# Two weight tiles of a convolution layer split by GpSimd, more convolution taps on VectorE and fewer on TensorE

## The chip, the cores and the metric

The kernel runs on one core of a Trainium2 chip. The metric is the device time of one execution in microseconds (us). The engines are TensorE (PE in the profile, its weight loads PEld), VectorE (DVE), ScalarE (ACT), GpSimd (POOL) and SyncE (SP), which here only issues transfers.

## The reference, cut to what matters

The model is a two-layer decoder trunk over 272 prompt positions and 32 sample positions (304 columns, D = 1024). Layer 0 is a pooling mixer and a dense SwiGLU, layer 1 is the Conformer convolution module below and a top-2-of-8 mixture of experts.

```python
def conv_module(x, prev, w1, b1, dw, dwb, lng, lnb, w2, b2):
    h = jnp.dot(x, w1) + b1                 # first pointwise layer, 1024 -> 2048
    a, gt = jnp.split(h, 2, axis=-1)
    u = a * jax.nn.sigmoid(gt)
    ext = jnp.concatenate([prev.astype(u.dtype), u], axis=1)
    c = lax.conv_general_dilated(ext, dw.astype(ext.dtype)[:, None, :], window_strides=(1,), padding='VALID',
                                 dimension_numbers=('NWC', 'WIO', 'NWC'), feature_group_count=D_MODEL)
    c = layer_norm(c + dwb, lng, lnb)       # 31 taps for each of the 1024 channels
    y = jnp.dot(jax.nn.silu(c), w2) + b2    # second pointwise layer
    return y.astype(x.dtype), ext[:, -CONV_CTX:]
```

## The kernel before, in words

**Split products.** Features lie on the 128 partitions in blocks (8 blocks make D), positions along the free axis. Each matrix product of the layers is made from three products of rounded parts: a weight tile of 128x2048 lands in `raw`, ScalarE rounds it to `w_hi` (`hi(t)`, L699), VectorE makes the low half `w_lo = raw - w_hi` in place over `raw` (`lo(t)`, L1357), and TensorE multiplies high by high, high by low and low by high. `raw` is a ring of slots, `w_hi` has 6 buffers. Weight tiles are numbered by t; `T_W1` = 33 to 40 are the eight tiles of the first pointwise layer, 41 to 44 those of the second, from 45 on the experts' tiles follow. The semaphore `hi_ready` counts finished high halves, `split_ready` finished low halves, `tile_used` tiles that TensorE has finished with.

**The stage around the change** has four turns, i = 0 to 3, of two tiles each (values and gates of two feature blocks, L1091 on TensorE). At the end of a turn ScalarE makes the sigmoids of the two gate blocks (L852) and VectorE writes two blocks of u (`uext`, L1585 and L1587). In the gaps between, VectorE splits the next tiles and convolves: `tap(q)` adds one tap of block q to `cacc` (the first of a block is L1536, the others L1540), and `convolve(pair, n)` makes n taps of both blocks of a pair. VectorE's order is written out by hand in this loop; each engine runs its own program in order and waits only for semaphores.

**The convolution is divided.** Blocks 0 to 3 (pairs 0 and 1) are convolved by VectorE alone, 31 taps each. Blocks 4 to 6 are convolved by TensorE with diagonal matrices (L1168): three matmuls for a tap, whose diagonals ScalarE builds beforehand (L789, L791, high and low). Block 7, `SHARED`, is divided by taps: TensorE makes taps 0 to 15, VectorE taps 16 to 30, and VectorE adds the two sums at the end (L1609). `DIAGS` lists TensorE's seven sets of diagonals, the last is that of the shared block. The samples' columns are convolved by VectorE in four groups of eight small operations (L1561).

**What follows.** When both have finished, TensorE sums the blocks for the mean of a normalization (L1030), VectorE subtracts it (L1432), ScalarE squares (L743), and so on to the second pointwise layer, the router and the experts. GpSimd's program at this point waits for the variance before the stage, zeroes the first columns of `uext` (L623), and then waits until the router to issue indirect transfers (L638, L629, L633).

The lines of VectorE's turn that matter most:

```python
            for i in range(NW1 // 2):
                if i < NW1 // 2 - 1:
                    lo(T_W1 + 2 * i + 2)
                    if i:
                        convolve(0, 4)
                    lo(T_W1 + 2 * i + 3)
                if i == NW1 // 2 - 1:
                    uc_low(0)
                    uc_low(1)
                if i:
                    convolve(0, 4 if i < NW1 // 2 - 1 else 12)
```

Of the kernel before, what the change touches and what calls it, by code (L numbers as in the profile page):

```python
# [29 lines left out]
ALU = mybir.AluOpType  # L30
# [5 lines left out]
HIGH = 6  # L36
# [5 lines left out]
def build_trunk(nc, x_prompt, x_sample, state_pool, state_conv, meta, pool_w, pool_scale, conv_w1,  # L42
# [5 lines left out]
    KC = D // P  # L48
# [5 lines left out]
    TAPS = conv_dw.shape[1]  # L54
# [17 lines left out]
    T_W1 = 3 * NJ  # L72
    NW1 = 2 * D // TW
# [13 lines left out]
    def raw_slot(t):  # L87
        if t >= T_MOE:
            return (t - T_MOE + DENSE) % RAW
        return t - T_W2 if t >= T_W2 else t % DENSE  # L90
# [9 lines left out]
    with ExitStack() as ctx:  # L100
# [18 lines left out]
        raw = [at(f"raw{i}", [P, 2048], F32, ring_at + 8192 * i) for i in range(RAW)]  # L119

        w_lo = [at(f"w_lo{i}", [P, 2048], F32R, ring_at + 8192 * i) for i in range(RAW)]
        w_hi = [at(f"w_hi{i}", [P, 2048], F32R, split_at + 8192 * i) for i in range(HIGH)]
# [71 lines left out]
        Q0 = KC - NPE  # L194
# [55 lines left out]
        def sem(name):  # L250
            return ctx.enter_context(nc.semaphore(name))
# [11 lines left out]
        u_stored = sem("u_stored")  # L263
        hi_ready = sem("hi_ready")
        split_ready = sem("split_ready")
        tile_used = sem("tile_used")
        consts_ready = sem("consts_ready")
        ctx_zeroed = sem("ctx_zeroed")
# [113 lines left out]
        def up_end(b):  # L382
# [40 lines left out]


        SHARED = KC - 1
        DIAGS = [(q, k0, min(k0 + 16, TAPS)) for q in range(Q0, KC) for k0 in (0, 16)
                 if q != SHARED or k0 == 0]
        EARLY = len(diag_at)

        def diag(j):  # L430
# [160 lines left out]
        def _(pool):  # L591
# [29 lines left out]

            pool.wait_ge(var_done, 2)
            pool.memset(uext[:, :, 0:CCTX], 0.0).then_inc(ctx_zeroed, 1)  # L623


            rows = bass.IndirectOffsetOnAxis
# [58 lines left out]
        def _(act):  # L685
# [96 lines left out]
            def diagonals(j, first, end):  # L782

                q, k0, k1 = DIAGS[j]
                n = k1 - k0
# [210 lines left out]
        def _(pe):  # L996
# [100 lines left out]
            for i in range(NJ):  # L1097
                for kind in range(2):
                    t = 2 * i + kind
# [3 lines left out]
                    for s in range(2 if t else 0):  # L1103
                        q = 2 * i + s
# [8 lines left out]
            for i in range(NJ):  # L1113
                t = T_DOWN + i
# [3 lines left out]
                for s in range(TR):  # L1118
                    for c in range(KC):
                        cols = slice(c * P, (c + 1) * P)  # L1120
                        for k, (w, x) in enumerate(((wh, h_hi), (wh, h_lo), (wl, h_hi))):
                            last = pe.matmul(ps[c][:, 0:NT], w[:, s, cols], x[i % 2][:, s, :],  # L1122
                                             start=(i == 0 and s == 0 and k == 0),
                                             stop=(i == NJ - 1 and s == TR - 1 and k == 2))
# [12 lines left out]
            for i in range(NW1 // 2):  # L1137
                for kind in range(2):
                    t = T_W1 + 2 * i + kind
                    pe.wait_ge(split_ready, t + 1)  # L1140
                    if t == T_W1:
                        last = feature_block((ps[0], ps[2]), NT, t, (0, 1), x_base=KC)
                    for s in range(2 if t > T_W1 else 0):
                        q = 2 * i + s
                        if q >= 4:
                            pe.wait_ge(u_done, q - 3)
                        last = feature_block((ps[2 * (q % 4) + kind],), NT, t, (s,))
                    last.then_inc(tile_used, 1)

            for j, (q, k0, k1) in enumerate(DIAGS):  # L1150
                c = q - Q0
                if j == 2:
                    pe.wait_ge(u_done, KC)
                    for k, (part, half) in enumerate(U_JOBS):
                        dst = ps[U_BANKS[k]]
                        for o in range(4):
                            f = 4 * half + o
                            src = uext[:, f, UP - CCTX:UP] if part == 0 else uext[:, f, UP:UEXT]
                            n = (CCTX, NS)[part]
                            last = pe.transpose(dst[0:n, o * P:(o + 1) * P], src, ident[:])  # L1160
                        last.then_inc(turned, 1)
                pe.wait_ge(uc_lo_done, c + 1)
                pe.wait_ge(diag_done, j + 1)
                dh, dl = diag(j)
                for k in range(k0, k1):
                    cols = slice((k - k0) * P, (k - k0 + 1) * P)
                    for m, (w, x) in enumerate(((dh, uc_hi), (dh, uc_lo), (dl, uc_hi))):
                        last = pe.matmul(ps[2 + c][:, 0:SEQ], w[:, cols], x[:, c, k:k + SEQ],  # L1168
                                         start=(k == 0 and m == 0),
                                         stop=(k == (15 if q == SHARED else TAPS - 1) and m == 2))  # L1170
                last.then_inc(diag_used, 1)
            pe.wait_ge(evac_a, A_U)
            norm(2)
# [1 line left out]
            for i in range(NW2):  # L1175
                t = T_W2 + i
# [14 lines left out]
            for k, (i, half) in enumerate(X_JOBS):  # L1191
                if k == 1:

                    pe.wait_ge(logits_out, 1)
                    for t in range(3):
                        m = OUT_ROWS[t]
# [148 lines left out]
        def _(dve):  # L1345
# [8 lines left out]
            def lo(t, n=None):  # L1354

                dve.wait_ge(hi_ready, t + 1 if n is None else n * TE + (t + 1))
                dve.tensor_tensor(w_lo[raw_slot(t)][:], raw[raw_slot(t)][:], w_hi[t % HIGH][:],  # L1357
                                  ALU.subtract).then_inc(split_ready, 1)


            for job, (i, half) in enumerate(IN_JOBS):
# [119 lines left out]
            for i in range(NJ):  # L1481
# [19 lines left out]
                for s in range(2):  # L1501
                    q = 2 * i + s
# [3 lines left out]
            for i in range(-1, NJ):  # L1506
                if 0 <= i < NJ - 1:
                    lo(T_DOWN + i + 2)
                if i + 1 < NJ:
                    k = (i + 1) % 2  # L1510
# [13 lines left out]

            dve.wait_ge(ctx_zeroed, 2)
            dve.wait_ge(tile_used, T_W1)
            FIRST_TAP = [0] * (KC - 1) + [16]
            taps_done = FIRST_TAP[:]
            convolved = []

# [15 lines left out]
            def convolve(pair, count):  # L1546

                for _ in range(count):
                    tap(2 * pair)
                    tap(2 * pair + 1)  # L1550
# [19 lines left out]
            for i in range(NW1 // 2):  # L1570
                if i < NW1 // 2 - 1:
                    lo(T_W1 + 2 * i + 2)
                    if i:
                        convolve(0, 4)
                    lo(T_W1 + 2 * i + 3)
                if i == NW1 // 2 - 1:
                    uc_low(0)
                    uc_low(1)
                if i:
                    convolve(0, 4 if i < NW1 // 2 - 1 else 12)  # L1580
                for s in range(2):
                    q = 2 * i + s
                    dve.wait_ge(sig_done, q + 1)
                    src = ps[2 * (q % 4)]
                    dve.scalar_tensor_tensor(out=uext[:, q, CCTX:UP], in0=src[:, 0:NPR], scalar=v(V_B1 + q),  # L1585
                                             in1=sg[s][:, 0:NPR], op0=ALU.add, op1=ALU.mult)
                    dve.scalar_tensor_tensor(out=uext_s[:, q, :, :],  # L1587
                                             in0=src[:, NPR:NT].rearrange("p (b j) -> p b j", b=SB), scalar=v(V_B1 + q),
                                             in1=sg[s][:, NPR:NT].rearrange("p (b j) -> p b j", b=SB),
                                             op0=ALU.add, op1=ALU.mult).then_inc(u_done, 1)  # L1590
                dve.wait_ge(u_done, 2 * i + 2)

            uc_low(2)
            uc_low(3)
            convolve(0, TAPS - taps_done[0])
            dve.wait_ge(conv_step, len(convolved))
            dve.tensor_copy(most[:], eps[:]).then_inc(rows_convolved, 2)
            for r in range(TAPS):
                convolve(1, 1)
                if r < TAPS - 16:  # L1600
                    tap(SHARED)
                if r % 8 == 0:
                    for c in range(KC):
                        sample_tap(c, r // 8)
# [11 lines left out]
            for i in range(NW2):  # L1616
                lo(T_W2 + 2 + i)
                dve.wait_ge(tile_used, T_W2 + i + 1)
                for s in range(2):
                    q = 2 * i + s  # L1620
# [304 lines left out]
```

## Time and profile before

| | us |
|---|---|
| median of 3 runs | 1245.68 (1245.18 to 1245.83) |
| the profiled execution, its own time | 1244.82 |
| its span in the trace | 1243.0 |
| TensorE busy | 1197.5 (96% of the span) |
| VectorE busy | 977.1 (79%) |
| ScalarE busy | 807.4 (65%) |
| GpSimd busy | 31.0 (2%) |
| mean granted clock of TensorE | 0.991 |

The times of the trace count from the start of the span. A share of busy time is a mean over stages with different limits; the stage around the change lies between 287 and 387 us. Idle time is given with the instruction that ended it, as far as the trace shows one.

### The profile page before, as it was taken

To read this page: it belongs to the slowest core of one execution; us is meant where nothing else is said; L and a number is where in the kernel's file an instruction comes from. 1 tells how busy PE (TensorE), PEld (TensorE's weight loads), DVE (VectorE), ACT (ScalarE), POOL (GpSimd) and SP (SyncE) were. 2 spreads that over 40 slices of the span, in tenths; PEclk is the share of its full clock that TensorE was granted. 3 is DMA by queue.
4 is the path that set the end of the run, shared out by engine and by line. 5 is a ranking of instruction groups with operands and counts; after the bars stand their busy time and mean duration, and the time that the engine had idled before them with its cause. 6 is when DMAs were issued, how large, how long until landed. Compare 5 with 4: busy or idle time off the path is not lost.

```text
span 1243.0 us, 16100 instructions
## 1 busy us (share of the span) xinstructions
PE 1197.5 (96%) x6538; PEld 1036.4 (83%) x6538; DVE 977.1 (79%) x918; ACT 807.4 (65%) x875; POOL 31.0 (2%) x43
## 2 busy tenths in 40 slices
PE   6899999999998979999999999999999999999995
PEld 4799999999997868888888888888888888888884
DVE  6787444447898579879889888888888888888886
ACT  4545654436496467777768768777777777777771
POOL 0000000000000000000000001001001001001000
PEclk9999999999999979999999999999999999999998
DMA  9144544442193349999999999999999999999991
GB/s 258 40 157 149 170 149 157 141 157 89 56 317 110 136 145 365 363 364 355 388 373 362 384 367 365 384 367 363 390 367 362 390 365 353 389 372 345 395 334 50
DMA packets 171533, 346.26 MB, mean 279 GB/s; under 512 B 7059, under 2 KB 59635, under 8 KB 171419
## 3 DMA queue, kind: packets, MB, share of 16 engines
q1 hardware_dynamic: 168515, 335.34, 75.3%
q0 software_dynamic: 2736, 9.19, 2.9%
q8 instruction: 54, 0.88, 0.3%
q10 hardware_dynamic: 199, 0.62, 0.2%
q14 instruction: 29, 0.23, 0.1%
HBM read 336.87 MB, written 10.44 MB: 279 GB/s over the span
## 4 chain that ended last, share of the span: by engine, by line
PE 86%; DVE 10%; ACT 2%; DMA 1%; issue 1%; POOLq 0%; SPq 0%; POOL 0%; DVEq 0%; ACTq 0%
PE bank L1259 39%; PE bank L1283 19%; PE bank L1091 18%; PE bank L1122 6%; DVE cacc L1540 3%; PE bank L1268 1%; DVE w_lo L1357 1%; PE bank L1030 1%; PE bank L1076 1%; DVE sg L1437 1%; DMA xg_rows<-rows_dram,row_in 1%; DMA xin<-in_x_prompt_dram 1%; ACT w_hi L699 0%; ACT sq L743 0%; DVE cacc L1561 0%
## 5 line engine op out<-in xcount | busy, mean ns | idle before, releaser
L1357 DVE TENSOR_TENSOR w_lo<-raw,w_hi 128x2048 fp32r<-128x2048 f32 x309 | 704.3, 2290 | 163.9 <-ACT w_hi L699 162.9
L699 ACT CAST w_hi<-raw 128x2048 fp32r<-128x2048 f32 x309 | 589.2, 1914 | 242.6 <-PE bank L1259 82.5
L1259 PE MATMUL bank<-w_hi,xg_hi 128*128 128x512 f32 (+1 forms) x768 | 293.3, 382 | 0.6 <-DVE xg_lo L1752 0.6
L1259 PE MATMUL bank<-w_lo,xg_hi 128*128 128x512 f32 (+1 forms) x768 | 289.6, 377 | 0.0
L1259 PE MATMUL bank<-w_hi,xg_lo 128*128 128x512 f32 (+1 forms) x768 | 289.4, 377 | 0.0
L1091 PE MATMUL bank<-x_hi,w_hi 128*128 128x304 f32 (+1 forms) x544 | 165.8, 305 | 6.9 <-DVE x_lo L1444 3.7
L1259 PEld LDWEIGHTS bank<-w_hi,xg_lo 128*128 128x128 f32 x768 | 144.8, 189 | 29.2
L1259 PEld LDWEIGHTS bank<-w_hi,xg_hi 128*128 128x128 f32 x768 | 144.8, 189 | 29.0 <-issue 1.0
L1259 PEld LDWEIGHTS bank<-w_lo,xg_hi 128*128 128x128 f32 x768 | 144.9, 189 | 27.9
L1091 PE MATMUL bank<-x_hi,w_lo 128*128 128x304 f32 (+1 forms) x544 | 164.1, 302 | 0.0
L1091 PE MATMUL bank<-x_lo,w_hi 128*128 128x304 f32 (+1 forms) x544 | 163.9, 301 | 0.0
L1283 PE MATMUL bank<-w_hi,ht_hi 128*128 128x512 f32 x352 | 140.1, 398 | 2.3 <-DVE ht_lo L1776 1.9
L1283 PE MATMUL bank<-w_lo,ht_hi 128*128 128x512 f32 x352 | 139.2, 396 | 0.0
L1283 PE MATMUL bank<-w_hi,ht_lo 128*128 128x512 f32 x352 | 139.2, 396 | 0.0
L1091 PEld LDWEIGHTS bank<-x_hi,w_hi 128*128 128x128 f32 x544 | 102.2, 188 | 8.9 <-issue 6.3
L1091 PEld LDWEIGHTS bank<-x_hi,w_lo 128*128 128x128 f32 x544 | 102.7, 189 | 0.0
L1091 PEld LDWEIGHTS bank<-x_lo,w_hi 128*128 128x128 f32 x544 | 102.2, 188 | 0.1
L1283 PEld LDWEIGHTS bank<-w_hi,ht_hi 128*128 128x128 f32 x352 | 66.1, 188 | 19.6 <-DVE ht_lo L1776 4.3
L1283 PEld LDWEIGHTS bank<-w_hi,ht_lo 128*128 128x128 f32 x352 | 66.1, 188 | 16.0
L1283 PEld LDWEIGHTS bank<-w_lo,ht_hi 128*128 128x128 f32 x352 | 66.1, 188 | 15.3
L1122 PE MATMUL bank<-h_hi,w_hi 128*128 128x304 f32 x176 | 54.4, 309 | 1.9 <-DVE h_lo L1514 1.9
L1540 DVE SCALAR_TENSOR_TENSOR cacc<-uext,vec,cacc 128x256 f32<-128x256 f32 x134 | 54.0, 486 | 0.0
(220 smaller groups left out, 1076.8 us busy)
## 6 DMA issues: line engine op xcount, KB each, us to landing
raw<-in_moe_w_gate_dram SPq DMA_DIRECT2D x88, 1024.0 KB, 6.6
raw<-in_moe_w_up_dram SPq DMA_DIRECT2D x88, 1024.0 KB, 7.1
raw<-in_moe_w_down_dram SPq DMA_DIRECT2D x88, 1024.0 KB, 6.8
raw<-in_conv_w_dram SPq DMA_DIRECT2D x12, 1024.0 KB, 5.2
raw<-in_ffn_w_gate_dram SPq DMA_DIRECT2D x11, 1024.0 KB, 5.4
raw<-in_ffn_w_up_dram SPq DMA_DIRECT2D x11, 1024.0 KB, 5.4
raw<-in_ffn_w_down_dram SPq DMA_DIRECT2D x11, 1024.0 KB, 4.8
sums_dram<-acc SPq DMA_DIRECT2D x3, 512.0 KB, 3.3
```

The source lines that it names most:

```text
L699: act.copy(w_hi[t % HIGH][:], raw[raw_slot(t)][:]).then_inc(hi_ready, 1)
L1030: last = pe.matmul(ps[0][:, 0:n], mean_mat[:], z(c), start=(c == first), stop=(c == end))
L1076: last = pe.matmul(ps[1][:, 0:n], mean_mat[:], sq[:, c, 0:n], start=(c == 0), stop=(c == KC - 1))
L1091: last = pe.matmul(bank[:, 0:n], w[:, c, cols], x[:, c, 0:n], start=(c == 0 and k == 0), stop=(c == KC - 1 and k == 2))
L1122: last = pe.matmul(ps[c][:, 0:NT], w[:, s, cols], x[i % 2][:, s, :], start=(i == 0 and s == 0 and k == 0), stop=(i == NJ - 1 and s == TR - ...
L1259: done = pe.matmul(bank[:, 0:w], x[:, f, :], m[:, c, :], start=(f == 0 and k == 0), stop=(f == KC - 1 and k == 2))
L1268: done = pe.transpose(ps[4 + j % 2][:, s * P:(s + 1) * P], hn[:, s * P:(s + 1) * P], ident[:])
L1283: done = pe.matmul(ps[6 + half][:, :], x[:, i * TR + s, :], w[:, s, cols], start=(j == 0 and i == 0 and s == 0 and k == 0), stop=(j == NB ...
L1357: dve.tensor_tensor(w_lo[raw_slot(t)][:], raw[raw_slot(t)][:], w_hi[t % HIGH][:], ALU.subtract).then_inc(split_ready, 1)
L1437: link(dve.reciprocal(rs[:, 0:n], rs[:, 0:n]))
L1540: ins = dve.scalar_tensor_tensor(out=out, in0=src, scalar=v(V_DW + KC * k + q), in1=out, op0=ALU.mult, op1=ALU.add)
```

## The change

GpSimd makes the low halves of tiles 38 and 40 (`POOL_TILES`) with one subtraction of 128x2048 each, and TensorE waits for `pool_split` there; VectorE's next `lo` counts `split_ready` up by two, so that the count stays that of the tiles. In the turns i = 1 and 2 VectorE makes 4 and then 7 taps of pair 0 where it made 4, a low half and 4; in turn 3 it makes the remaining 9 of pair 0 and the first 4 of pair 1 where it made 12 of pair 0. Of the shared block TensorE has 8 taps (`SHARE`) and VectorE 23, and the last set of diagonals is half as large. The taps of pair 0 behind the last turn are gone.

```diff
--- before.py
+++ after.py
@@ -263,6 +263,7 @@
         u_stored = sem("u_stored")
         hi_ready = sem("hi_ready")
         split_ready = sem("split_ready")
+        pool_split = sem("pool_split")
         tile_used = sem("tile_used")
         consts_ready = sem("consts_ready")
         ctx_zeroed = sem("ctx_zeroed")
@@ -423,8 +424,11 @@
 
 
         SHARED = KC - 1
-        DIAGS = [(q, k0, min(k0 + 16, TAPS)) for q in range(Q0, KC) for k0 in (0, 16)
+        SHARE = 8
+        DIAGS = [(q, k0, SHARE if q == SHARED else min(k0 + 16, TAPS)) for q in range(Q0, KC) for k0 in (0, 16)
                  if q != SHARED or k0 == 0]
+
+        POOL_TILES = (T_W1 + 5, T_W1 + 7)
         EARLY = len(diag_at)
 
         def diag(j):
@@ -621,6 +625,10 @@
 
             pool.wait_ge(var_done, 2)
             pool.memset(uext[:, :, 0:CCTX], 0.0).then_inc(ctx_zeroed, 1)
+            for t in POOL_TILES:
+                pool.wait_ge(hi_ready, t + 1)
+                pool.tensor_tensor(w_lo[raw_slot(t)][:], raw[raw_slot(t)][:], w_hi[t % HIGH][:],
+                                   ALU.subtract).then_inc(pool_split, 1)
 
 
             rows = bass.IndirectOffsetOnAxis
@@ -1137,7 +1145,10 @@
             for i in range(NW1 // 2):
                 for kind in range(2):
                     t = T_W1 + 2 * i + kind
-                    pe.wait_ge(split_ready, t + 1)
+                    if t in POOL_TILES:
+                        pe.wait_ge(pool_split, POOL_TILES.index(t) + 1)
+                    else:
+                        pe.wait_ge(split_ready, t + 1)
                     if t == T_W1:
                         last = feature_block((ps[0], ps[2]), NT, t, (0, 1), x_base=KC)
                     for s in range(2 if t > T_W1 else 0):
@@ -1167,7 +1178,7 @@
                     for m, (w, x) in enumerate(((dh, uc_hi), (dh, uc_lo), (dl, uc_hi))):
                         last = pe.matmul(ps[2 + c][:, 0:SEQ], w[:, cols], x[:, c, k:k + SEQ],
                                          start=(k == 0 and m == 0),
-                                         stop=(k == (15 if q == SHARED else TAPS - 1) and m == 2))
+                                         stop=(k == (SHARE - 1 if q == SHARED else TAPS - 1) and m == 2))
                 last.then_inc(diag_used, 1)
             pe.wait_ge(evac_a, A_U)
             norm(2)
@@ -1355,7 +1366,7 @@
 
                 dve.wait_ge(hi_ready, t + 1 if n is None else n * TE + (t + 1))
                 dve.tensor_tensor(w_lo[raw_slot(t)][:], raw[raw_slot(t)][:], w_hi[t % HIGH][:],
-                                  ALU.subtract).then_inc(split_ready, 1)
+                                  ALU.subtract).then_inc(split_ready, 2 if t - 1 in POOL_TILES else 1)
 
 
             for job, (i, half) in enumerate(IN_JOBS):
@@ -1524,7 +1535,7 @@
 
             dve.wait_ge(ctx_zeroed, 2)
             dve.wait_ge(tile_used, T_W1)
-            FIRST_TAP = [0] * (KC - 1) + [16]
+            FIRST_TAP = [0] * (KC - 1) + [SHARE]
             taps_done = FIRST_TAP[:]
             convolved = []
 
@@ -1572,12 +1583,15 @@
                     lo(T_W1 + 2 * i + 2)
                     if i:
                         convolve(0, 4)
-                    lo(T_W1 + 2 * i + 3)
+                    else:
+                        lo(T_W1 + 2 * i + 3)
                 if i == NW1 // 2 - 1:
                     uc_low(0)
                     uc_low(1)
                 if i:
-                    convolve(0, 4 if i < NW1 // 2 - 1 else 12)
+                    convolve(0, 7 if i < NW1 // 2 - 1 else TAPS - taps_done[0])
+                if i == NW1 // 2 - 1:
+                    convolve(1, 4)
                 for s in range(2):
                     q = 2 * i + s
                     dve.wait_ge(sig_done, q + 1)
@@ -1592,12 +1606,12 @@
 
             uc_low(2)
             uc_low(3)
-            convolve(0, TAPS - taps_done[0])
             dve.wait_ge(conv_step, len(convolved))
             dve.tensor_copy(most[:], eps[:]).then_inc(rows_convolved, 2)
             for r in range(TAPS):
-                convolve(1, 1)
-                if r < TAPS - 16:
+                if taps_done[2] < TAPS:
+                    convolve(1, 1)
+                if r < TAPS - SHARE:
                     tap(SHARED)
                 if r % 8 == 0:
                     for c in range(KC):
```

## Rows read from the trace of the kernel before

**Rows 1.** Chain that ended last, 284 to 410 us: start us, us, what.

```profile
...
287.35 54.26 PE bank L1091 x384
...
349.44 9.51 DVE cacc L1540 x24
...
382.76 4.13 PE bank L1030 x16
```

**Rows 2.** Busy us of PE, PEld, DVE, ACT, POOL by stretch; clock, DMA.

```profile
...
287.00:341.00 54.00, 53.65 (x381) 53.51 (x382) 46.20 (x90) 30.36 (x59) 0.00 (x0) 1.00 0.25 79
341.00:382.00 41.00, 41.00 (x348) 40.80 (x346) 39.66 (x122) 35.71 (x108) 0.00 (x0) 1.00 0.71 247
...
450.00:460.00 10.00, 6.47 (x40) 5.21 (x40) 6.30 (x24) 1.75 (x5) 0.95 (x1) 0.51 0.65 220
```

**Rows 3.** TensorE's timeline, first and last diagonal matmuls: start, us, what.

```profile
...
341.44 0.28 PE L1168 MATMUL bank<-uc_hi,diag_h 128*128 128x256 f32 x1
...
342.39 0.28 PE L1168 MATMUL bank<-uc_hi,diag_l 128*128 128x256 f32 x1
...
382.00 0.28 PE L1168 MATMUL bank<-uc_hi,diag_l 128*128 128x256 f32 x1
```

**Rows 4.** Timeline of VectorE, 306 to 383 us: start, us, what, idle before.

```profile
...
306.35 0.73 DVE L1536 TENSOR_SCALAR cacc<-uext,vec 128x256 f32<-128x256 f32 x2
306.99 2.46 DVE L1540 SCALAR_TENSOR_TENSOR cacc<-uext,vec,cacc 128x256 f32<-128x256 f32 x6
309.37 2.29 DVE L1357 TENSOR_TENSOR w_lo<-raw,w_hi 128x2048 fp32r<-128x2048 f32 x1
...
315.31 0.50 DVE L1585 SCALAR_TENSOR_TENSOR uext<-bank,vec,sg 128x272 f32<-128x272 f32 x1 [0.48 <-ACT sg L852]
...
317.58 2.29 DVE L1357 TENSOR_TENSOR w_lo<-raw,w_hi 128x2048 fp32r<-128x2048 f32 x1 [1.02 <-ACT w_hi L699]
319.79 3.25 DVE L1540 SCALAR_TENSOR_TENSOR cacc<-uext,vec,cacc 128x256 f32<-128x256 f32 x8
...
328.75 0.50 DVE L1585 SCALAR_TENSOR_TENSOR uext<-bank,vec,sg 128x272 f32<-128x272 f32 x1 [0.34 <-ACT sg L852]
...
330.87 9.59 DVE L1540 SCALAR_TENSOR_TENSOR cacc<-uext,vec,cacc 128x256 f32<-128x256 f32 x24
342.19 0.50 DVE L1585 SCALAR_TENSOR_TENSOR uext<-bank,vec,sg 128x272 f32<-128x272 f32 x1 [1.73 <-ACT sg L852]
...
382.39 0.15 DVE L1606 COPY mv<-eps 128x1 f32<-128x1 f32 x1
```

**Rows 5.** Timeline of ScalarE in the same stretch.

```profile
...
306.49 1.91 ACT L699 CAST w_hi<-raw 128x2048 fp32r<-128x2048 f32 x1 [2.46 <-DMA raw<-in_conv_w_dram]
...
319.88 1.91 ACT L699 CAST w_hi<-raw 128x2048 fp32r<-128x2048 f32 x1 [2.40 <-DMA raw<-in_conv_w_dram]
...
368.58 4.78 ACT L791 ACTIVATE diag_l<-ident,dw_lo 128x128 fp32r<-128x128 f32 x16
376.57 0.47 ACT L835 ACTIVATE cacc<-bank,vec 128x256 f32<-128x256 f32 x1 [2.50 <-PE bank L1168]
```

**Rows 6.** Groups of GpSimd by shape: count, busy us, mean ns, idle before.

```profile
...
L623 POOL MEMSET uext<- 128x240 f32 x1 | 0.3, 298 | 279.4 <-PE bank L1076 279.4
L605 POOL TENSOR_SCALAR_AFFINE_SELECT before<-before 128x128 f32<-128x128 f32 x1 | 0.3, 292 | 0.1
...
L597 POOL MEMSET pext<- 128x120 f32 x1 | 0.2, 196 | 0.0
```

**Rows 7.** Timeline of TensorE where its clock rises again.

```profile
...
463.11 0.63 PE L1259 MATMUL bank<-w_hi,xg_hi 128*128 128x512 f32 x1
463.54 0.55 PE L1259 MATMUL bank<-w_lo,xg_hi 128*128 128x512 f32 x1
...
464.39 0.40 PE L1259 MATMUL bank<-w_lo,xg_hi 128*128 128x512 f32 x1
464.62 0.40 PE L1259 MATMUL bank<-w_hi,xg_lo 128*128 128x512 f32 x1
```

## The prediction

> **What bounds the kernel now.** I read the chain of waits first, then the stretches of busy time, then each engine's timeline in the stage. In the chain [rows 1] the reader is to see that TensorE sets the end up to the last tile of the first pointwise layer (384 matmuls, 54.26 us from 287.35) and that VectorE's taps set it from there to 382.76, when the mean's matmuls start. The stretches [rows 2] show why it is a near tie: from 341 to 382 TensorE is busy all 41.0 us and VectorE 39.66 us, both at the full granted clock. The timelines give the two ends. TensorE's last diagonal matmul starts at 382.00 and takes 0.28, so it ends at 382.28 [rows 3]; VectorE's taps end where the small copy begins, at 382.39 [rows 4]. So neither alone is worth anything: a gain here needs both to end earlier, and it is the smaller of the two gains. The turns before 341 bind TensorE: 54.26 us for eight tiles is 6.78 us a tile, so tile 38, the sixth, is wanted at 287.35 + 5 x 6.78 = 321.3 and tile 40 at 334.8. VectorE has idle time in these turns [rows 4], GpSimd does nothing at all [rows 2].
>
> **TensorE's part.** It loses 8 taps of three matmuls. From 341.44 to 342.39 there are eight steps [rows 3], 0.119 us each, so 24 matmuls are 2.8 us and its end moves from 382.28 to 379.5. The last set of diagonals has 16 scalings in place of 32; the second half alone, 16, took 4.78 us and was over by 373.4, TensorE came to this set only at 376.5 [rows 5], so ScalarE's saving is hidden and counts for nothing. The earlier release of the experts' first slots counts for nothing either: these tiles are wanted only after the router.
>
> **VectorE's part, if GpSimd does not disturb it.** A tap costs 0.396 us (24 in 9.51 [rows 1]); the first two taps of a pair take 306.99 - 306.35 = 0.64 together [rows 4]. Turn 1: the eight taps end at 309.37, 14 more take 5.54 and end at 314.9, before the sigmoid lets VectorE go on at 315.31. Turn 2: the low half ends at 319.79, 22 taps take 8.71 and end at 328.5, before 328.75. Turn 3: from 330.87, 18 taps of pair 0 (7.13) and the first eight of pair 1 (0.64 + 6 x 0.396 = 3.02) end at 341.0, before 342.19. So no turn becomes longer, and the two low halves of 2.29 us are paid out of it and out of idle time of 0.48, 0.34 and 1.73 us. Behind the last turn there were 6 + 62 + 15 = 83 taps; now there are 54 of pair 1 and 23 of the shared block, 77. Six taps less are 2.4 us: VectorE's end moves from 382.39 to 380.0. TensorE's 379.5 is earlier, so the stage would gain 2.4 us, and nothing behind it binds differently: the mean, the square and the second layer follow in the same chain.
>
> **GpSimd's part.** Its program stands at a wait with nothing queued but transfers that come some 100 us later, so queuing behind the two subtractions costs nothing. Tile 38 is rounded at 306.49 + 1.91 = 308.4 and tile 40 at 321.8 [rows 5]; each leaves 13 us until TensorE wants it. The trace has no operation of GpSimd with two tiles as input. From below: two fills, 0.298 us for 240 columns and 0.196 for 120 [rows 6], give 0.85 ns a column, 1.8 us for 2048. From above: the selection of 128 columns takes 0.292 [rows 6]; without some 0.09 of fixed time (0.196 - 120 x 0.85 ns) that is 1.55 ns a column, 3.3 us for one operand and up to 6.4 if the second is read after the first. I take 4.6 us, close to the middle of these last two (4.8) and to sixteen selections (4.7). All of them fit into 13 us, so the wait that TensorE now has for GpSimd costs nothing unless GpSimd is held up by over 8 us.
>
> **What decides: whether the two run side by side.** While GpSimd subtracts, VectorE runs nothing but taps and low halves, each with two operands in the same memory as GpSimd's. No row here shows such a pair together: in the stage GpSimd has 0.00 us [rows 2]. The two ends are that they do not touch (0) and that each excludes the other, so that VectorE stands still for the whole of both subtractions (2 x 4.6 = 9.2 us). I take exclusion, as the likelier of two untested ends, and it is by far the larger term. Of the 9.2 us, idle time of the turns absorbs 0.4 (314.9 to 315.31), 1.0 (the low half that waits for its rounding until 317.58 [rows 4]), 0.2 (328.5 to 328.75) and 1.2 (341.0 to 342.19): 2.8 us. 6.4 us remain, and VectorE ends at 380.0 + 6.4 = 386.4, 4.0 later than before. The point from which the sign turns: 2 x H - 2.8 = 2.4, so H = 2.6 us of standstill for each tile.
>
> The Trainium skill's page "SBUF — State Buffer", section "Who interferes with whom", speaks against this change: VectorE operations with two inputs in this memory contend with a GpSimd operation that reads it, and the one that issues second blocks until the first has finished. Its page "GPSIMD Engine Reference", section 3.1, gives 4497 ns for a two-input operation of 2048 columns, an estimate of 9.0 us for both tiles. By this rule and this price the sum would be that of exclusion, 0.2 us smaller; no trace so far shows either.
>
> **What is late next under exclusion.** In the delayed turns the u blocks come 4 to 7 us later; ScalarE's later diagonals slip by as much but were ready several us early (the last set by 3 us, and it is now 4.7 us shorter). TensorE never waits for them, ends at 379.5, and then idles 7.2 us before the mean's 16 matmuls. Before the experts, where TensorE was busy for 6.47 of 10 us, the granted clock had a mean of 0.51, the 1.2 GHz level [rows 2]; there a matmul came each 0.43 us (463.11 to 463.54) and at 2.4 GHz each 0.23 (464.39 to 464.62) [rows 7], 1.85 times as long. The 4.13 us of mean matmuls [rows 1] at the lower level would take 3.5 us more; between 0 and 3.5 I take 2.0, as the clock may rise inside the group.
>
> **The sum.** -2.4 + 6.4 + 2.0 = +6.0 us: a span of 1249.0, an execution of 1244.82 + 6.0 = 1250.8. The profiled execution is 0.9 below the median of the runs, so against the median it is 1245.7 + 6.0 = 1251.7.
>
> **The rivals.**
> *Side by side.* GpSimd's reads do not hold VectorE up. For it: nothing in the trace shows GpSimd disturbing VectorE. Against it: nothing there reads two tiles at once on both. Then the gain is 2.4 us, 1243.3: not slower, the other side of my forecast. It decides when the standstill is under 2.6 us a tile.
> *GpSimd has to wait for VectorE's gaps.* Taps follow each other closely (0.396 us apart), so a waiting GpSimd may come in only where VectorE stops. Tile 38 then runs from 314.9 to 319.5, under the writes of u, which read a bank and one tile; the low half at 317.58 slips 1.9 us, 22 taps end at 330.45, the writes of u end at 331.7, and tile 40 runs from 330.45 to 335.05, 0.2 us after TensorE wants it. The remaining work starts at 335.05 and reaches the last writes of u at 346.1 in place of 342.19, 3.9 late. VectorE ends at 383.9, 1.5 after the old end: 1247.2, and up to 1250.7 with the slower clock. An even sharing of the reads, in which both become slower, lands in the same place.
> *The subtraction is shorter or longer than I take.* With exclusion and 1.8 us there is a loss of 0.9 and a gain of 1.5 in all; with 6.4 us a loss of 10.0 and +7.6, with the clock +11.1.
>
> **How the numbers follow.** A measurement of this kernel tells about 0.2%, 2.5 us, from no change. Exclusion has 0.50, gaps or sharing 0.14, side by side 0.36. Exclusion is slower by over 2.5 us in nearly all its cases (0.47), gaps in a third (0.05): slower 0.52. Side by side stands 0.1 us short of the bound, so four in ten of it count as faster (0.15) and the rest as same (0.21); with gaps (0.09) and a short standstill (0.03) same has 0.33. The forecast is 1251.7; its own range is 1247 (one operand's 3.3 us, full clock) to 1255 (clock low throughout, a longer subtraction). The range for 8 in 10 reaches to side by side, from 1242.8 to 1254.8.
>
> **What would show it.** Right: in turns 1 and 2 one tap or low half of VectorE stretched to about 4.6 us, or a hole as long before it, beside each subtraction of GpSimd; the last writes of u near 349 in place of 342.19; taps to about 386; an idle TensorE from 379.5, with the granted clock under 1.00 in the mean's matmuls. Wrong: taps still 0.396 apart beside GpSimd, last writes of u at 342.2, both engines ready near 380. A subtraction of over 13 us would be wrong in another way: TensorE would then wait for tile 38 or 40, and the loss would stand before 341.

## The result, and the profile after

The changed kernel takes 1249.74 us (median of 9 runs, 1246.52 to 1252.69) and the kernel before, run on the same chips, 1245.18 (9 runs, 1244.39 to 1246.4). The ratio is 1.0036, with a 95% interval of 1.0024 to 1.0047: slower by 4.5 us. The profiled execution has a span of 1248.8 us and 1250.65 in all, 5.8 us more than that of before.

The chain that ended last, from 284 to 412 us in the changed kernel, passes to VectorE earlier and stays there longer:

```profile
...
286.94 27.37 PE bank L1099 x192
...
317.19 4.04 DVE w_lo L1368
321.22 13.07 DVE cacc L1551 x22
...
336.41 7.13 DVE cacc L1551 x18
...
382.57 1.59 DVE cacc L1551 x4
...
384.61 6.46 PE bank L1038 x16
```

Against [rows 1] the reader sees three things. TensorE leaves the chain after four tiles (27.37 us), not eight. A low half that took 2.29 us is in it with 4.04, and 22 taps that would take 8.7 with 13.07. The 16 matmuls of the mean, 4.13 us before, take 6.46.

GpSimd's two subtractions and VectorE's timeline beside them:

```profile
...
308.23 10.84 POOL L630 TENSOR_TENSOR w_lo<-raw,w_hi 128x2048 fp32r<-128x2048 f32 x1 [25.44 <-ACT w_hi L707]
321.56 4.92 POOL L630 TENSOR_TENSOR w_lo<-raw,w_hi 128x2048 fp32r<-128x2048 f32 x1 [2.49 <-ACT w_hi L707]
```

```profile
...
306.57 8.01 DVE L1551 SCALAR_TENSOR_TENSOR cacc<-uext,vec,cacc 128x256 f32<-128x256 f32 x20
...
317.19 4.04 DVE L1368 TENSOR_TENSOR w_lo<-raw,w_hi 128x2048 fp32r<-128x2048 f32 x1 [1.05 <-ACT w_hi L707]
321.14 13.15 DVE L1551 SCALAR_TENSOR_TENSOR cacc<-uext,vec,cacc 128x256 f32<-128x256 f32 x22
...
346.48 0.50 DVE L1599 SCALAR_TENSOR_TENSOR uext<-bank,vec,sg 128x272 f32<-128x272 f32 x1
...
384.25 0.15 DVE L1620 COPY mv<-eps 128x1 f32<-128x1 f32 x1
```

```profile
...
321.94 4.83 DVE L1551 SCALAR_TENSOR_TENSOR cacc<-uext,vec,cacc 128x256 f32<-128x256 f32 x1
```

The last row is the only instruction of VectorE that runs from 322 to 326: one tap of 4.83 us among taps of 0.48, beside GpSimd's second subtraction of 4.92. Beside the first one, which has a record of 10.84 us, no tap is longer than usual (20 in 8.01). The low half behind these taps starts at 317.19, GpSimd is done at 319.07, and the low half ends 2.16 us after that, at 321.23: it stood still until GpSimd was done and then took about its own 2.29 us. The last writes of u begin at 346.48 in place of 342.19 [rows 4].

The stretches (busy us of PE, PEld, DVE, ACT, POOL, then TensorE's granted clock) and TensorE's last diagonal matmul:

```profile
...
287.00:341.00 54.00, 54.00 (x384) 53.84 (x385) 47.23 (x87) 26.55 (x46) 15.75 (x2) 1.00 0.25 79
341.00:382.00 41.00, 38.01 (x321) 37.60 (x319) 40.96 (x124) 34.63 (x105) 0.00 (x0) 1.00 0.75 257
382.00:387.00 5.00, 2.39 (x5) 1.85 (x6) 4.80 (x12) 0.00 (x0) 0.00 (x0) 0.55 1.04 385
```

```profile
...
378.73 0.28 PE L1179 MATMUL bank<-uc_hi,diag_l 128*128 128x256 f32 x1
384.61 1.78 PE L1038 MATMUL bank<-cacc,mean_mat 128*128 128x288 f32 x3 [5.60 <-DVE mv L1621]
```

TensorE has finished at 379.0 and waits 5.6 us for VectorE; its granted clock is 1.00 up to 382, as in [rows 2], and has a mean of 0.55 from 382 to 387, for the most part the 1.2 GHz level.

### The profile page after: what moved, and what is told of

Its sections match the earlier page's. It is cut to its first block, busy times and chain, and to the rows that moved or that the text cites. A ratio compares the mean times of both kernels' runs of the same rounds, so it can differ in the third digit from the quotient of the medians.

```text
span 1248.8 us, 16045 instructions
## 1 busy us (share of the span) xinstructions
PE 1198.6 (96%) x6514; PEld 1037.0 (83%) x6514; DVE 982.1 (79%) x924; ACT 802.4 (64%) x859; POOL 47.0 (4%) x45
## 4 chain that ended last, share of the span: by engine, by line
PE 84%; DVE 12%; ACT 2%; DMA 1%; issue 1%; POOLq 0%; POOL 0%; DVEq 0%; ACTq 0%
PE bank L1270 39%; PE bank L1294 19%; PE bank L1099 16%; PE bank L1130 6%; DVE cacc L1551 4%; DVE w_lo L1368 2%; PE bank L1279 1%; PE bank L1038 1%; PE bank L1084 1%; DVE sg L1448 1%; DMA xg_rows<-rows_dram,row_in 1%; ACT w_hi L707 1%; ACT sq L751 0%; DVE cacc L1572 0%; PE bank L1018 0%
## 5 line engine op out<-in xcount | busy, mean ns | idle before, releaser
L1551 DVE SCALAR_TENSOR_TENSOR cacc<-uext,vec,cacc 128x256 f32<-128x256 f32 x142 | 61.4, 521 | 0.0
```

The costliest lines, as they stand in the source:

```text
L1551: ins = dve.scalar_tensor_tensor(out=out, in0=src, scalar=v(V_DW + KC * k + q), in1=out, op0=ALU.mult, op1=ALU.add)
```

## The experiments

All are compared by one length that the start of the stage does not shift: from the first matmul of tile 33 to the copy behind VectorE's last tap. In the kernel before it is 382.39 - 287.35 = 95.04 us, in the changed one 384.25 - 286.94 = 97.31, so VectorE is 2.3 us later. A span in the table is that of one execution. Since the times of the changed kernel alone lie 6.2 us apart, the readings rest on these lengths and not on the spans.

| kernel | VectorE's end against before | mean's matmuls, us | span or ratio |
|---|---|---|---|
| before | 0 | 4.1 | 1243.0 |
| changed | +2.3 | 6.5 | ratio 1.0036 (1.0024 to 1.0047) |
| the same, second profile | +2.4 | 6.2 | span 1245.7 |
| one column on GpSimd | -2.4 | 4.1 | ratio 0.997 (0.9958 to 0.9981) |
| fill on GpSimd | -2.4 | 4.1 | span 1240.7 |
| copy on GpSimd | -2.2 | 4.1 | span 1240.7 |
| tile 40 alone | +0.5 | 6.9 | span 1246.7 |
| eight pieces | +2.6 | 5.8 | span 1247.4 |
| one subtraction at the start | +2.3 | 6.1 | ratio 1.0014 (1.0004 to 1.0025) |
| asked in mid-stream | +1.0 | 6.6 | span 1249.3 |
| asked at the gaps | +1.5 | 6.7 | span 1246.9 |
| matmuls to keep TensorE busy | +2.3 | 4.1 | ratio 1.0023 (1.0011 to 1.0036) |
| 16 taps of the shared block again | -0.5 | 4.1 | ratio 1.0005 (0.9994 to 1.0015) |
| idle time filled, no GpSimd | -1.6 | 4.1 | ratio 0.9993 (0.9983 to 1.0002) |

**Is it GpSimd's reading?** First its work taken away:

```diff
-                pool.tensor_tensor(w_lo[raw_slot(t)][:], raw[raw_slot(t)][:], w_hi[t % HIGH][:],
+                pool.tensor_tensor(w_lo[raw_slot(t)][:, 0:1], raw[raw_slot(t)][:, 0:1], w_hi[t % HIGH][:, 0:1],
                                    ALU.subtract).then_inc(pool_split, 1)
 ...
-                wh, wl = wide(w_hi[t % HIGH]), wide(w_lo[raw_slot(t)])
+                wh, wl = wide(w_hi[t % HIGH]), wide(w_hi[t % HIGH] if t in POOL_TILES else w_lo[raw_slot(t)])
```

> The changed kernel, but GpSimd subtracts one column of each of its two tiles and TensorE takes the high half in place of the low one there, so the low halves of tiles 38 and 40 are left out. Exclusion: without GpSimd's long reads VectorE's taps stay 0.396 us apart, they end 2.4 us earlier than in the kernel before (near 380), TensorE does not idle and keeps its clock, and the time is 2.4 us below that of the kernel before (0.2% faster). Rival (the new order of taps and TensorE's shorter part cost the time, not GpSimd): it stays 4 to 6 us above the kernel before.

```profile
...
308.76 8.00 DVE L1551 SCALAR_TENSOR_TENSOR cacc<-uext,vec,cacc 128x256 f32<-128x256 f32 x20
...
321.59 8.80 DVE L1551 SCALAR_TENSOR_TENSOR cacc<-uext,vec,cacc 128x256 f32<-128x256 f32 x22
```

```profile
...
310.31 6.51 POOL L630 TENSOR_TENSOR w_lo<-raw,w_hi 128x1 fp32r<-128x1 f32 x1 [25.34 <-ACT w_hi L707]
```

The taps are back at 20 in 8.00 and 22 in 8.80 us, VectorE's end is 2.42 us earlier than before, and the time 0.3% lower (the 2.4 us are 0.2%, at the edge of the interval). So the order of the taps and TensorE's eight taps, with two low halves that no engine makes, gain what the sum without GpSimd said; the loss is that of GpSimd's subtractions. The record of 6.51 us for one column ends at 316.82, 0.06 us behind the last tap of turn 1 (308.76 + 8.00 = 316.76), which matters below. Then its work with no input, and with one:

```diff
+                pool.memset(w_lo[raw_slot(t)][:].bitcast(F32), 0.0).then_inc(pool_split, 1)   # the fill
+                pool.tensor_copy(w_lo[raw_slot(t)][:], raw[raw_slot(t)][:]).then_inc(pool_split, 1)   # the copy
```

> The changed kernel, but GpSimd fills its two tiles with zeros, which writes 128x2048 and reads nothing; the low halves of tiles 38 and 40 are left out. Exclusion between two readers: no tap or low half of VectorE is stretched, taps end near 380, span 2.4 us below that of the kernel before. Rival (any long work of GpSimd in this memory stops VectorE): a tap or low half is stretched by about the length of the fill, 1.8 us, twice, less the idle time of the turns, and the span is about that of the kernel before.

```profile
...
308.88 1.82 POOL L630 MEMSET w_lo<- 128x2048 f32 x1 [25.35 <-ACT w_hi L706]
322.25 1.81 POOL L630 MEMSET w_lo<- 128x2048 f32 x1 [11.56 <-ACT w_hi L706]
```

Two fills of 1.8 us in the middle of VectorE's taps cost nothing: the end is 2.43 us earlier, as with one column.

> The changed kernel, but GpSimd copies its two tiles in place (one operand read, 128x2048) and does not subtract; tiles 38 and 40 have the whole weight in place of the low half. Exclusion: the copy still reads, so VectorE is stretched by about the copy's length (2 to 3.3 us for one operand) where GpSimd comes in among taps, less where it comes in at a gap; span between 2.4 below and 2 above the kernel before, and below the changed kernel. Rival (only an operation with two operands on GpSimd disturbs VectorE): no stretch at all, span 2.4 below the kernel before.

```profile
...
308.63 8.29 POOL L630 CAST w_lo<-raw 128x2048 fp32r<-128x2048 f32 x1 [25.26 <-ACT w_hi L706]
322.00 2.18 POOL L630 CAST w_lo<-raw 128x2048 fp32r<-128x2048 f32 x1 [5.09 <-ACT w_hi L706]
```

```profile
...
L1550 DVE SCALAR_TENSOR_TENSOR cacc<-uext,vec,cacc x22: 470/475/2114, 320.0 to 329.9; 128x256 f32<-128x256 f32 x22
```

The copy, 2.18 us when it comes in at once, stretches one tap to 2.11 us. The 1.6 us that this costs are nearly all taken up by idle time behind it (0.2 and 1.2), so the end is 2.2 us earlier than before. It is reading that excludes, with one operand as with two.

**Whole operations, or shared reads?**

```diff
+                for k in range(8):
+                    cols = slice(256 * k, 256 * k + 256)
+                    last = pool.tensor_tensor(w_lo[raw_slot(t)][:, cols], raw[raw_slot(t)][:, cols], ...)
+                last.then_inc(pool_split, 1)
```

> The changed kernel, but GpSimd subtracts each tile in eight pieces of 256 columns. If each operation excludes the other engine's for its own length: no tap of some 4.8 us any more, but in turn 2 several taps longer by about one piece (0.6 to 1.2 us) each, with the sum of a whole subtraction or more, and the same or a later end of VectorE. Rival (pieces slip in between taps): taps unchanged and the end near 380.

```profile
...
310.43 6.94 POOL L632 TENSOR_TENSOR w_lo<-raw,w_hi 128x256 fp32r<-128x256 f32 x8 [25.30 <-ACT w_hi L710]
323.96 7.17 POOL L632 TENSOR_TENSOR w_lo<-raw,w_hi 128x256 fp32r<-128x256 f32 x8 [6.58 <-ACT w_hi L710]
```

```profile
...
308.94 11.89 DVE L1554 SCALAR_TENSOR_TENSOR cacc<-uext,vec,cacc 128x256 f32<-128x256 f32 x20
...
324.30 12.66 DVE L1554 SCALAR_TENSOR_TENSOR cacc<-uext,vec,cacc 128x256 f32<-128x256 f32 x22
```

20 taps take 11.89 us and 22 take 12.66: 3.9 more in either turn, with no tap over 0.96 us. Taps twice as long as usual, about half a us more each, make up a standstill of nearly a whole subtraction (4.4), in slices. With this kernel even turn 1 pays in full, and the end is the latest of all.

```diff
+                n = 2048 if t == T_W1 + 7 else 1
+                pool.tensor_tensor(w_lo[raw_slot(t)][:, 0:n], raw[raw_slot(t)][:, 0:n], ...)
```

> The changed kernel, but of tile 38 GpSimd subtracts one column only and TensorE takes the high half there (its low half is left out); tile 40 as changed. One tap of turn 2 stretched by 4.4 us, of which 1.4 of idle time is absorbed: VectorE's end 3.0 us later than without GpSimd's work, 0.6 later than in the kernel before. Rival (both engines share the reads and slow each other evenly): no single long tap, many slightly longer ones.

```profile
...
308.78 0.20 POOL L631 TENSOR_TENSOR w_lo<-raw,w_hi 128x1 fp32r<-128x1 f32 x1 [25.29 <-ACT w_hi L708]
322.25 4.76 POOL L631 TENSOR_TENSOR w_lo<-raw,w_hi 128x2048 fp32r<-128x2048 f32 x1 [13.27 <-ACT w_hi L708]
```

```profile
...
L1552 DVE SCALAR_TENSOR_TENSOR cacc<-uext,vec,cacc x22: 467/475/4835, 320.1 to 332.8; 128x256 f32<-128x256 f32 x22
```

One tap of 4.83 us, the median of all 0.475: not shared, but one behind the other. +0.5 against +0.6 expected.

**Who waits for whom?** In turn 1 GpSimd was held up, in turn 2 VectorE was. My first theory was a start-up of GpSimd's first subtraction.

```diff
+            pool.wait_ge(consts_ready, N_CONSTS)
+            pool.tensor_tensor(warm[:], eps[:], eps[:], ALU.subtract)
             pool.wait_ge(var_done, 2)
```

> The changed kernel with one subtraction of one column on GpSimd at the very start. Theory: GpSimd's first subtraction of the kernel has some 6 us of start-up in which it holds nothing (one column took 6.51 us the first time and 0.48 the second), and that is why tile 38 left VectorE's taps alone. Then tile 38 now takes under 5 us from 308.4, one tap of turn 1 is stretched to about 4.8 us, the next low half is back at 2.29 us, and VectorE's taps end 1 to 2 us later than in the changed kernel. Rival (a close stream of taps holds GpSimd off): tile 38 still takes 10.8 us and the low half behind it 4.0 us, nothing changes.

```profile
...
308.16 11.08 POOL L635 TENSOR_TENSOR w_lo<-raw,w_hi 128x2048 fp32r<-128x2048 f32 x1 [25.16 <-ACT w_hi L710]
321.57 4.68 POOL L635 TENSOR_TENSOR w_lo<-raw,w_hi 128x2048 fp32r<-128x2048 f32 x1 [2.33 <-ACT w_hi L710]
```

Tile 38 still has 11.08 us, and VectorE's end is that of the changed kernel: the theory fell. What fits is the end of the taps: here the last tap of turn 1 ends at 314.75 and the record at 319.24, in the changed kernel at 314.58 and 319.07, both 4.49 us later, a subtraction's own length. GpSimd stood still until VectorE's stream of taps ended. The single column above, which ended 0.06 us behind the last tap, fits the same, and the kernel with tile 40 alone, whose first column took 0.20 us, shows no start-up. The ratio, 1.0014, is below the changed kernel's 1.0036, and the intervals hardly meet, although the stage is the same within 0.4 us: the time has a part that does not come from the stage (see the last point on the prediction). The second profile of the changed kernel was to show whether that is chance.

> The changed kernel as it is, a second profile. If what GpSimd meets is the same in each execution: tile 38 held off again (10.8 us, the low half behind it 4.0 us) and one tap of turn 2 at 4.8 us. If it is chance: a long tap in turn 1 as well, or none in turn 2, and an end of VectorE that differs by 1 to 4 us.

```profile
...
307.92 10.95 POOL L630 TENSOR_TENSOR w_lo<-raw,w_hi 128x2048 fp32r<-128x2048 f32 x1 [25.35 <-ACT w_hi L707]
321.35 4.62 POOL L630 TENSOR_TENSOR w_lo<-raw,w_hi 128x2048 fp32r<-128x2048 f32 x1 [2.48 <-ACT w_hi L707]
```

The same in each part (and a tap of 4.91 us). Then the moment of asking was moved, with one of these two lines in each kernel:

```diff
                 pool.wait_ge(hi_ready, t + 1)
+                pool.wait_ge(conv_step, 12 if t == T_W1 + 5 else 34)   # in mid-stream
+                pool.wait_ge(sig_done, 3 if t == T_W1 + 5 else 5)      # at the gaps
```

> The changed kernel, but GpSimd also waits for the 12th tap in all (turn 1) and the 34th (turn 2), so that it asks at the same point behind a tap, in the middle of the stream, in both turns. If the point behind a tap decides whether GpSimd comes in: both turns go alike. If the turn decides: in turn 1 GpSimd is held off to the end of the taps (a record of some 4 + 4.5 = 8.5 us, no long tap, the low half behind it at 4.0), in turn 2 one tap is stretched to 4.8.

```profile
...
313.57 8.30 POOL L631 TENSOR_TENSOR w_lo<-raw,w_hi 128x2048 fp32r<-128x2048 f32 x1 [28.02 <-DVE cacc L1552]
328.91 8.33 POOL L631 TENSOR_TENSOR w_lo<-raw,w_hi 128x2048 fp32r<-128x2048 f32 x1 [7.04 <-DVE cacc L1552]
```

```profile
...
319.98 4.03 DVE L1369 TENSOR_TENSOR w_lo<-raw,w_hi 128x2048 fp32r<-128x2048 f32 x1 [1.05 <-ACT w_hi L708]
323.94 8.79 DVE L1552 SCALAR_TENSOR_TENSOR cacc<-uext,vec,cacc 128x256 f32<-128x256 f32 x22
...
333.93 3.99 DVE L1579 TENSOR_TENSOR uc_lo<-uext,uc_hi 128x286 fp32r<-128x286 f32 x2
```

Both turns go alike: 8.30 and 8.33 us, no long tap, and what is long is VectorE's first operation with two operands behind the writes of u. So 4 to 5 us into a stream GpSimd waited for its end, and in turn 2 of the changed kernel it had asked within 0.5 us of the stream's beginning and came in before the third tap. No rule follows: some 1.5 us into the stream of turn 1 the subtraction, the copy and one column were held off, but the eight pieces and, in the kernel with tile 40 alone, one column (0.20 us) were not; 2.0 and 2.2 us into the stream of turn 2 the copy and, with tile 40 alone, a whole subtraction came in. What decides at the moment of asking stays open. What the records show without exception is where such a record ends: in all eight records of a whole subtraction that was held off, it lies 4.49 to 4.51 us behind the last tap of the stream.

> The changed kernel, but GpSimd waits for the third and the fifth sigmoid, so that both subtractions begin while VectorE writes u from the banks. Exclusion of whole operations: no long tap; the low half behind turn 1 at about 4.0 us, and behind turn 2 the low half of a convolution block (0.46 us) stretched to 3 to 3.5 us; VectorE's taps end 1.2 us earlier than in the changed kernel, still later than without GpSimd. Rival (writes of u are held up too, or nothing is): the writes stretched by 4 us, or an end near 380.

```profile
...
315.29 4.63 POOL L631 TENSOR_TENSOR w_lo<-raw,w_hi 128x2048 fp32r<-128x2048 f32 x1 [32.24 <-ACT sg L861]
328.71 6.56 POOL L631 TENSOR_TENSOR w_lo<-raw,w_hi 128x2048 fp32r<-128x2048 f32 x1 [8.79 <-ACT sg L861]
```

```profile
...
317.47 4.60 DVE L1369 TENSOR_TENSOR w_lo<-raw,w_hi 128x2048 fp32r<-128x2048 f32 x1 [1.04 <-ACT w_hi L708]
...
331.98 3.97 DVE L1579 TENSOR_TENSOR uc_lo<-uext,uc_hi 128x286 fp32r<-128x286 f32 x2
```

The second request came 2.1 us before the taps of turn 2 ended, and it too was held off to their end (its record ends 4.49 us behind the last tap). The low half takes 4.60 us and the pair of small ones 3.97; the writes of u (0.49 us), which read a bank that TensorE writes its sums to and one tile, are not held up. The end is 1.54 later than before, 0.7 earlier than in the changed kernel, where 1.2 was expected. This is the rival of the gaps made on purpose, which gave 1.5 for VectorE's end.

**The clock's part.**

```diff
             pe.wait_ge(evac_a, A_U)
+            keep_busy(18)
             norm(2)
```

> The changed kernel with 18 small matmuls (128x128, some 4.3 us) on TensorE behind the diagonal matmuls, where it idled for 5 us. If the lower clock in the mean's matmuls is a part of the loss: those 16 matmuls take 4.1 us in place of 6.5, and the time falls by 2 to 3 us against the changed kernel, to some 2 us above the kernel before. Rival (the clock's part is not there, or is given back later before the experts): no change, 4 to 5 us above the kernel before. VectorE's stretches stay as they were.

```profile
...
385.56 4.13 PE bank L1038 x16
```

VectorE is as late as in the changed kernel, the mean's matmuls are back at 4.13 us. The ratio falls from 1.0036 to 1.0023, 1.6 us, where 2 to 3 were expected. The intervals overlap, and the kernel with one subtraction at the start, whose mean's matmuls still took 6.1 us, has a lower ratio (1.0014). So the saving of 2.3 us is shown in the profile; the times do not show it.

```diff
-        SHARE = 8
+        SHARE = 16
```

> The changed kernel with one part undone: TensorE has 16 taps of the shared block again, VectorE 15. Theory: VectorE's end comes 3.2 us earlier than in the changed kernel, near 381.5, TensorE's last diagonal matmul ends near 382.3 and does not idle, the clock stays at 1.00, and the time is that of the kernel before within 0.1%. Rival (GpSimd's standstill costs wherever TensorE ends): slower than the kernel before by 2 us or more.

```profile
...
PE bank L1179 <- ACT diag_l L799: 1.7, 1, 1.7
```

VectorE's copy begins at 381.56, as expected. TensorE ends at 383.9, not 382.3: it waits 1.7 us for the last diagonals, since ScalarE is late with them behind the delayed u. With eight taps this set is half as long and that wait does not exist. Counted from the first matmul of tile 33, the mean's matmuls begin 1.5 us later than in the kernel before. The rival's 2 us lie outside the interval of the time, and the time is not told apart from that of the kernel before (0.9994 to 1.0015); but that the standstill costs nothing when TensorE has 16 taps is not shown, since through ScalarE it still delays TensorE.

**A version without GpSimd.**

```diff
+        SHARE = 12
 ...
-                    lo(T_W1 + 2 * i + 2)
+                    if i == 2:
+                        convolve(0, 1)
+                    lo(T_W1 + 2 * i + 2)
 ...
-                    convolve(0, 4 if i < NW1 // 2 - 1 else 12)
+                    convolve(0, 5 if i == 1 else 4 if i < NW1 // 2 - 1 else TAPS - taps_done[0])
+                if i == NW1 // 2 - 1:
+                    convolve(1, 1)
 ...
-            convolve(0, TAPS - taps_done[0])
 ...
```

> The kernel before with its low halves on VectorE, GpSimd unused: VectorE only fills the idle time of the turns (9 pairs of taps in turn 1, 1 + 8 in turn 2, 13 of pair 0 and 1 of pair 1 in turn 3), and TensorE has 12 taps of the shared block, not 16. If the stage is a tie of VectorE and TensorE: eight taps leave the tail (3.0 us) and four come to it (1.6), so VectorE ends 1.4 us earlier; TensorE loses 12 matmuls, 1.4 us. Time 1.4 us (0.1%) below the kernel before. Rival (the turns have no room, since the writes of u come later): no change or slower.

The stage is 1.6 us shorter at VectorE's end and the mean's matmuls stay at 4.1 us, but 0.9993 (0.9983 to 1.0002) is not told apart from 1. It beats the changed kernel, whose interval begins at 1.0024 (that of the same stage with one subtraction at the start at 1.0004); that it beats the kernel before is not shown.

## Why the prediction was right, point by point

The direction and the mechanism were right: exclusion of two readers, a late VectorE, an idle TensorE, a lower clock in the mean's matmuls. The time forecast was 1251.7 and measured 1249.7: 6.0 us more than before against 4.5, from a median of before that was then 0.5 lower. The exclusion cost 1.7 us less than forecast and the clock 0.3 more, which makes 4.6; what follows the stage, which the sum put at nothing, moves by up to 4 us from one profile to another. That the profiled execution, with 5.8 us, comes so close to 6.0 is luck. The last writes of u, forecast near 349, began at 346.48, and VectorE ended at 384.25 where 386.4 was forecast.

*TensorE's part.* Forecast 2.8 us earlier; 379.0 from a start 0.4 earlier is 2.9. Right. That ScalarE's smaller set is worth nothing holds for the kernel as changed; with VectorE held up and 16 taps it is worth 1.7 us.

*VectorE's part without GpSimd.* Forecast -2.4; measured -2.42 and -2.43. Right.

*GpSimd's length.* Forecast 4.6; measured 4.92 and 4.62 in the two profiles. Right. The Trainium skill's page "GPSIMD Engine Reference", section 3.1, has 4497 ns for a two-input addition of 2048 columns; the 4.49 us behind the last tap agree, the records are a little longer.

*Exclusion.* Forecast 9.2 us of standstill, 6.4 after idle time; measured 1.75 (4.04 - 2.29) and 4.4 (13.07 - 8.7), of which 0.2 and 1.2 were idle, so 4.7. This is the term that was mis-sized. Its premise, that VectorE stands still for the whole of both, holds for tile 40 alone; tile 38 behaved as in the rival of the gaps, and 2.6 us of it lay under VectorE's idle time, the writes of u and the wait behind them (314.58 to 317.19). The Trainium skill's page "SBUF — State Buffer", section "Who interferes with whom", has it that the one that issues second blocks, that a GpSimd operation which only writes does not contend, and that a VectorE operation with at most one input from this memory, outside the faster modes that use its second ports, does not; the tap of 4.83 us, the fills without a cost and the writes of u at 0.49 us agree. That a waiting GpSimd operation lets tap after tap of VectorE pass, for over 6 us in turn 1 (308.23 to 314.58), is more than that section says.

*The clock.* Forecast 2.0; measured 6.46 - 4.13 = 2.3, and 1.7 to 2.8 in the other profiles in which TensorE idled here. Right.

*What follows the stage.* I had said that nothing behind it binds differently. The chain is the same, but the clock at the first expert is not. The kernel before, the changed one and its second profile, TensorE's timeline from the first expert matmul:

```profile
...
460.41 0.77 PE L1259 MATMUL bank<-w_hi,xg_hi 128*128 128x512 f32 x1 [0.64 <-DVE xg_lo L1752]
```

```profile
...
465.12 0.77 PE L1270 MATMUL bank<-w_hi,xg_hi 128*128 128x512 f32 x1 [0.64 <-DVE xg_lo L1766]
...
470.80 0.60 PE L1270 MATMUL bank<-w_lo,xg_hi 128*128 128x512 f32 x1
471.23 0.40 PE L1270 MATMUL bank<-w_hi,xg_lo 128*128 128x512 f32 x1
```

```profile
...
464.73 0.47 PE L1270 MATMUL bank<-w_hi,xg_hi 128*128 128x512 f32 x1 [0.69 <-DVE xg_lo L1766]
465.04 0.39 PE L1270 MATMUL bank<-w_lo,xg_hi 128*128 128x512 f32 x1
```

The first expert begins 4.7 us later than before and, in the second profile, 4.3 later. That is VectorE's 2.3 and 2.4 and the mean's 2.3 and 2.1, less 0.4 and 0.6 by which the stage began earlier, and 0.5 and 0.4 that the gather of the experts' rows took longer (7.56 and 7.50 us against 7.07; why is open). From there the matmuls of the kernel before came at 0.43 us until about 463.9 [rows 7], those of the changed kernel until 471.2, those of its second profile hardly at all. With 0.43 us for a matmul in place of 0.23, each us at the lower level loses 0.46 us, so 6.1 us of it in place of 3.5 cost 1.2 more, and 0.3 us in place of 3.5 gain 1.5: 4.7 + 1.2 = 5.9 and 4.3 - 1.5 = 2.8, against spans 5.8 and 2.7 above that of before. So the profiled execution's 5.8 contains 1.2 us of this kind, where the other profile gained 1.5, and this is one source of the wide spread of the changed kernel's runs (6.2 us against 2.0). It is not bound to the change: from the first expert matmul to the end of the span, where all fourteen programs are alike, their profiles take from 779.7 us (one subtraction at the start) to 783.7 (the changed kernel, and that with 16 taps), and the kernel before takes 782.6. So what the stage costs is read from its own lengths, 4.6 and 4.5 us for VectorE and the mean in the two profiles of the changed kernel; that the median of the times says the same is in part chance.

## What to carry to other kernels

Before moving an operation that reads SBUF (the on-chip memory that the tiles lie in) from VectorE to GpSimd, look at what VectorE runs meanwhile. Here that was work with two inputs from SBUF, and 2.29 us of work taken off VectorE each time bought a standstill of 1.75 and 4.4. A fill by GpSimd cost nothing, and VectorE's writes of u, with one input from a bank, were not held up. And where two engines end a stage within a tenth of a us of each other, a delay of one can cost twice: here TensorE's 5.6 us of waiting was followed by 2.3 us more in the mean's matmuls at the lower clock.

## What the runs showed that I had not expected

A close stream of VectorE's taps, one each 0.396 us, held a waiting GpSimd operation off to its very end (10.8 to 11.1 us for 4.5 to 4.9 of work, and 8.3 twice when it asked later), though a request at the beginning of a stream came in before the third tap, and one 2.2 us into a stream came in too. Two executions of one kernel reached the first expert within 0.4 us of each other and came out 3.1 us apart; how long the clock stayed at its lower level there accounts for 2.7 of it.
